# Combining expert rows inside the last expert, and projections ahead of the gates: a two-layer decoder step on one Trainium2 core

## The chip, the cores and the metric

The kernel runs on one core of one Trainium2 chip. Its engines are TensorE (PE), VectorE (DVE), ScalarE (ACT), GpSimd (POOL) and SyncE (SP). SP issues the loads of the weights, POOL the other transfers. The metric is the device time of one execution in microseconds, as the median of several runs.

## The reference, cut to what matters

520 tokens (512 of a prompt, 8 samples) pass two layers of width 1024. Each layer is a mixer, a feed-forward part and an input embedding p, with RMS norms around them. In the second layer the feed-forward part is a mixture of eight experts, of which each token uses two:

```python
gates = sum(one_hot(top_i) * top_p)            # two of 8 per token
for e in range(8):
    y = y + gates[..., e:e+1] * swiglu(h, wg[e], wu[e], wd[e])
x = x + rms_norm(y, norm_ffn_post)
gate = sigmoid(rms_norm(x, norm_ple) @ ple_w_gate)
x = x + gate * (p @ ple_w_proj)
```

All inputs are float32. The change is in the last lines: how y is put together for the tokens in layer 1, and when p @ ple_w_proj is computed.

## The kernel before, in words

Activations are kept transposed: 128 partitions by eight chunks of 520 tokens (x, acc). Dense matrix products split both factors into a rounded part and a remainder in PE's fast float32 format (whi and wlo by split(), h_hi and h_lo) and add three products; a matmul of 128 x 260 in that form is one instruction. A plain float32 matmul is two.

**The experts (layer 1).** The tokens of each expert are gathered into 160 slots (CAP): POOL scatters token rows to DRAM (xslot) by index (idxu), and loads the 160 rows of each expert back. Every expert has 30 weight slabs (E_SLABS): 11 pairs of gate and up, 8 of down. SP streams the slabs into a ring of 10; load number m waits until PE has read slab m - 10. In experts_by_slots() PE runs slab after slab with slab_slots(); gate slabs leave PSUM by ACT's Silu, up slabs by DVE's product (gs). A slab may start when the slab four before it has left its PSUM bank. For each down slab d, ACT or DVE copies the result to ytb, PE transposes it back to rows in rows_out() (lines 974 and 975), and rows_act() or rows_dve() copy the rows to ys0 and ys1; POOL stores them to DRAM (yslot). In the same place slots_in() transposes the rows of the next expert. If an expert had more rows than slots, experts_by_all() would run in place of this.

**After the last expert.** SP waits for the last slab, then loads two projection slabs (in_ple_w_proj) and the first two gate slabs. ACT and DVE split them, project_p() runs eight times on PE, and take_p() copies each result. Meanwhile POOL waits until all rows are stored and gathers, for five tiles t of 128 tokens (the last has 8), two rows per token (lines 649 and 650). ACT scales the first row by its gate (ctok), DVE adds the second, PE transposes the tile (line 1060), DVE adds it to acc in add_rows(). Only two tiles fit: POOL's third gather waits for DVE's first sum. Then ACT loads the table for logarithm and exponential, squares the eight chunks of acc, PE forms the means in norm(), root() makes the factor rn by Ln and Exp. normed() adds acc * rn to x on DVE and POOL, new_h() and low_h() make the next h, eight gate slabs run (slab()), and gated() multiplies by the projections.

Each engine runs its program in order, so the order of the work is written out by hand: where one engine needs another's result, it waits on a semaphore for a count, and everything behind it on that engine waits as well. The names that matter below: moe_done counts slabs by PE, act_out and dve_out what left PSUM, yx_t row transposes, ys_act and ys_dve row copies, y_back gathers, cb_a, cb_b, cb_t and cb_acc the steps of the combine.

Of the kernel before, what the change touches and what calls it, by code (L numbers as in the profile page):

```python
# [59 lines left out]
NSLOT = NE * CAP  # L60
SLICES = (2, 0)
# [30 lines left out]
def build(nc, A, O):  # L92
    ctx = ExitStack()
    with ctx:
# [21 lines left out]
        sq_sum = z[:, 12]  # L116
# [16 lines left out]
        with nc.sbuf_tensor("yrow", [P, 2, 2, DM], f32) as yrow, nc.sbuf_tensor("ctok", [P, 2, DM], f32) as ctok:  # L133
            pass
        with nc.sbuf_tensor("gu_hi", [P, FCH, TOK], f32r) as gu_hi, \
                nc.sbuf_tensor("gu_lo", [P, FCH, TOK], f32r) as gu_lo:
            pass
# [15 lines left out]
        with nc.sbuf_tensor("ys1", [P, DM], f32) as ys1:  # L153
            pass
# [22 lines left out]
        slot0 = sb("slot0", [P, 5])  # L177
        rt_col = sb("rt_col", [P, 5])
# [12 lines left out]
        def view(region, at, *shape):  # L191
# [3 lines left out]
            v = region[:, at:at + n]  # L195
            if len(shape) == 2:
                v = v.rearrange("p (a b) -> p a b", b=shape[1])
# [38 lines left out]

        def hn(k):

            return hn_a[:, k] if k < 6 else hn_b[:, k - 6]
# [29 lines left out]
        def two(ap):  # L269
# [4 lines left out]
        yslot = nc.dram_tensor("yslot", (NSLOT + 1, DM), f32).ap()  # L274
# [41 lines left out]
        acc0 = sem("acc0")  # L316
        hx_t, hx_ok, x_zero, rt_oh, rt_cnt, rt_idx, xs_scat, xs_in, xg_t, pk = (
            sem(s) for s in ("hx_t", "hx_ok", "x_zero", "rt_oh", "rt_cnt", "rt_idx", "xs_scat", "xs_in", "xg_t", "pk"))
        rwx_ok, rt_raw, rt_r, htok_ok, in0_ok, all_h = (
            sem(s) for s in ("rwx_ok", "rt_raw", "rt_r", "htok_ok", "in0_ok", "all_h"))  # L320
# [6 lines left out]
        y_back = [sem("y_back0"), sem("y_back1")]  # L327
# [45 lines left out]
        def _(sp):  # L373
# [27 lines left out]
            for L in range(DEPTH):  # L401
# [33 lines left out]
                loads(b + 1, PLE_P - 1, (b + 1) % 2, lambda s, i: cut(A["ple_w_gate"][L], i * 2 + s), kcs("ple"))  # L435
# [8 lines left out]
        def _(pool):  # L444
# [29 lines left out]
            for L in range(DEPTH):  # L474
# [126 lines left out]
                if L == 0:  # L601
# [6 lines left out]
                    for n in range(2):  # L608
                        half = yslot[NSLOT:NSLOT + 1, n * (DM // 2):(n + 1) * (DM // 2)]
# [6 lines left out]
                if L:  # L616
                    pool.wait_ge(r_ready, 5 * L + 3)
                    pool.memset(ytb[:, :, :], 0.0)
                    pool.memset(acc[:, :, :], 0.0).then_inc(acc0, 1)
# [22 lines left out]
                    pool.wait_ge(y_stored, 32 * (NE + 1))  # L642

                    for t in range(5):
                        n = P if t < TT else NB
                        if t >= 2:
                            pool.wait_ge(cb_b, t - 1)
                        for k in range(2):
                            pool.indirect_dma_start(out=yrow[0:n, t % 2, k, :], out_offset=None, in_=yslot[:, :],
                                                    in_offset=bass.IndirectOffsetOnAxis(ap=idxu[0:n, t, k:k + 1], axis=0),  # L650
                                                    bounds_check=NSLOT, oob_is_err=False).then_inc(y_back[t % 2], 16)
# [8 lines left out]
        def _(pe):  # L660
# [11 lines left out]
            def mean_of_sum(N, between=None):  # L672

                pe.wait_ge(sq_used, N * DC + DC - 1)
                for a in range(2):
                    mm(aux[:, a, 0:HALF], bcol(C_MEAN), two(sq_sum)[:, a], True, False)
# [6 lines left out]

            def norm(N):
                for c in range(DC):
                    mean(N, c)
# [200 lines left out]
            for L in range(DEPTH):  # L887
# [26 lines left out]
                if L:  # L914
                    pe.wait_ge(rwx_ok, 1)
# [13 lines left out]
                    pe.wait_ge(rt_raw, 1)  # L929
# [12 lines left out]
                    pe.wait_ge(rt_oh, 1)  # L942
# [26 lines left out]
                    def rows_out(e, d):  # L969

                        pe.wait_ge((act_out, dve_out)[d % 2], (e * E_SLABS + 2 * FCH + d) // 2 + 1)
                        if d >= 2:
                            pe.wait_ge((ys_act, ys_dve)[d % 2], e * DC // 2 + d // 2)
                        nc.tensor.transpose(aux[:, 2 + d % 2, 0:P], ytb[:, d % 2, 0:P], ident)  # L974
# [1113 lines left out]
```

## Time and profile before

| what | us |
|---|---|
| median of 3 runs | 1812.45 |
| lowest and highest | 1810.30, 1812.48 |
| the profiled execution | 1810.67 |
| its span, first to last instruction | 1808.9 |
| PE busy in the span | 1722.9 |
| ACT, DVE busy | 473.2, 579.6 |

The profiled execution is the one that all rows are from; its time is its span and 1.8 us around it. Times in rows are microseconds from the start of the span. Busy times of PE are modelled, and instructions overlap in it by their drains, so steps are better read from start to start.

### The profile page before, as it was taken

The numbers are of one execution on the slowest core, as the hardware profiler recorded it, in microseconds if no ns is written. First come the engines' busy times: TensorE is split into PE (matmuls) and PEld (weight loads), VectorE is DVE, ScalarE is ACT, GpSimd is POOL, SyncE is SP. The second block draws the span as 40 slices with busy tenths as digits, with TensorE's granted clock in tenths as the row PEclk, the third lists the DMA queues.
The fourth block names the chain that finished last, engine by engine and source line by source line (L and its number), as shares of the span: only waits on it lengthen the run. The fifth ranks groups of instructions, "written<-read, shape, count | busy, mean of one in ns | idle before, by whom it ended". The sixth has DMA issues, their size and how long they took to land.

```text
span 1808.9 us, 29442 instructions
## 1 busy us (share of the span) xinstructions
PE 1722.9 (95%) x12618; PEld 1619.7 (90%) x12618; DVE 579.6 (32%) x921; ACT 473.2 (26%) x836; POOL 258.1 (14%) x327
## 2 busy tenths in 40 slices
PE   7999998999999998899999799999999999999668
PEld 7877998999999997897789689999999999999658
DVE  3444535443344334643535500110101011010155
ACT  5232544222122334432334400110101101010242
POOL 5642211000000003054310220000000000000210
PEclk9999999999999999999999869999999999999879
DMA  4345361232222323223533257668686776965502
GB/s 164 83 86 117 76 207 59 93 102 97 77 88 91 113 64 98 70 72 89 111 77 107 92 177 258 225 226 279 198 289 216 244 249 205 300 195 197 168 17 90
DMA packets 70231, 260.69 MB, mean 144 GB/s; under 512 B 9849, under 2 KB 10369, under 8 KB 70097
## 3 DMA queue, kind: packets, MB, share of 16 engines
q1 hardware_dynamic: 56736, 219.52, 36.9%
q0 software_dynamic: 13376, 39.45, 8.3%
q8 instruction: 92, 1.51, 0.4%
q14 instruction: 27, 0.21, 0.0%
HBM read 237.20 MB, written 21.96 MB: 143 GB/s over the span
## 4 chain that ended last, share of the span: by engine, by line
PE 91%; DVE 4%; ACT 2%; DMA 1%; issue 1%; POOL 0%; ACTq 0%; DVEq 0%; SPq 0%; POOLq 0%
PE lin L662 77%; PE aux L662 12%; DVE h_lo L1536 1%; DVE zreg L1533 1%; PE aux L974 1%; DVE zreg L1536 1%; PE aux L966 1%; ACT h_hi L1098 1%; DMA yrow<-yslot,idxu 0%; DVE x L1533 0%; PE aux L975 0%; ACT htok L1098 0%; PE aux L965 0%; DMA wreg<-in_w_in_slabs 0%; DVE wlo L1533 0%
## 5 line engine op out<-in xcount | busy, mean ns | idle before, releaser
L662 PE MATMUL lin<-h_hi,whi 128*128 128x260 f32 x1616 | 432.8, 289 | 23.6 <-DVE h_lo L1536 23.6
L662 PE MATMUL lin<-h_lo,whi 128*128 128x260 f32 x1616 | 424.3, 284 | 0.0
L662 PEld LDWEIGHTS lin<-h_hi,whi 128*128 128x128 f32 x1616 | 308.3, 191 | 33.3 <-issue 27.6
L662 PE MATMUL lin<-h_hi,wlo 128*128 128x260 f32 x1616 | 327.8, 285 | 0.0
L662 PE MATMUL lin<-zreg,wreg 128*128 128x160 f32 x2304 | 321.6, 301 | 2.8 <-issue 2.8
L662 PEld LDWEIGHTS lin<-zreg,wreg 128*128 128x128 f32 x2304 | 317.2, 192 | 5.0 <-issue 4.9
L662 PEld LDWEIGHTS lin<-h_lo,whi 128*128 128x128 f32 x1616 | 307.8, 190 | 0.6
L662 PEld LDWEIGHTS lin<-h_hi,wlo 128*128 128x128 f32 x1616 | 251.2, 190 | 0.0
L1533 DVE TENSOR_TENSOR wlo<-wreg,whi 128x1024 fp32r<-128x1024 f32 (+1 forms) x140 | 180.7, 1291 | 96.3 <-ACT whi L1098 96.3
L1098 ACT ACTIVATE whi<-wreg 128x1024 fp32r<-128x1024 f32 (+1 forms) x140 | 152.1, 1090 | 74.5 <-DMA wreg<-in_ffn_w_down 26.8
L662 PE MATMUL lin<-region_b,wreg 128*128 128x160 f32 x1056 | 151.9, 300 | 0.0
L662 PEld LDWEIGHTS lin<-region_b,wreg 128*128 128x128 f32 x1056 | 145.0, 190 | 0.7
L1533 DVE TENSOR_TENSOR region_b<-zreg,lin 128x160 f32<-128x160 f32 x88 | 28.3, 322 | 342.7 <-PE lin L662 342.7
L1415 ACT ACTIVATE zreg<-lin 128x160 f32<-128x160 f32 x88 | 26.8, 304 | 347.7 <-PE lin L662 347.7
L1533 DVE TENSOR_TENSOR zreg<-lin,zreg 128x520 f32<-128x520 f32 x79 | 55.1, 698 | 156.5 <-PE lin L662 149.7
L472 POOL TENSOR_TENSOR x<-x,zreg 128x520 f32<-128x520 f32 x16 | 27.5, 1721 | 533.4 <-DVE zreg L1536 533.4
L662 PE MATMUL lin<-gu_hi,whi 128*128 128x260 f32 x352 | 92.0, 283 | 0.0
L662 PE MATMUL lin<-gu_lo,whi 128*128 128x260 f32 x352 | 91.9, 282 | 0.0
L640 POOL DMA_DIRECT2D yslot<-zreg x8 | 4.5, 561 | 606.2 <-DVE ys L1832 606.2
L662 PE MATMUL aux<-zreg,const 128*128 128x260 f32 (+1 forms) x216 | 66.3, 440 | 11.7 <-DVE h_lo L1536 8.0
L1098 ACT ACTIVATE zreg<-aux 128x128 f32<-128x128 f32 (+1 forms) x40 | 13.7, 342 | 224.4 <-PE aux L975 112.8
L662 PE MATMUL lin<-zreg,ring_more 128*128 128x160 f32 x512 | 72.2, 299 | 0.0
(280 smaller groups left out, 2281.8 us busy)
## 6 DMA issues: line engine op xcount, KB each, us to landing
wreg<-in_moe_w_gate SPq DMA_DIRECT2D x72, 512.0 KB, 4.2
wreg<-in_moe_w_up SPq DMA_DIRECT2D x72, 512.0 KB, 4.4
wreg<-in_moe_w_down SPq DMA_DIRECT2D x48, 704.0 KB, 5.2
wreg<-in_w_in_slabs SPq DMA_DIRECT2D x44, 512.0 KB, 3.5
wreg<-in_ffn_w_gate SPq DMA_DIRECT2D x22, 512.0 KB, 3.4
wreg<-in_ffn_w_up SPq DMA_DIRECT2D x22, 512.0 KB, 3.3
wreg<-in_ffn_w_down SPq DMA_DIRECT2D x16, 704.0 KB, 4.0
ring_more<-in_moe_w_down SPq DMA_DIRECT2D x16, 704.0 KB, 5.2
```

The lines of the kernel that those rows point to most:

```text
L472: pool.tensor_tensor(x[:, c], x[:, c], ut[:, 1], ALU.add).then_inc(x_pool, 1)
L640: pool.dma_start(yslot[e * CAP:e * CAP + P, :], ys0).then_inc(y_stored, 16)
L662: return nc.tensor.matmul(out, lhsT, rhs, start=start, stop=stop)
L966: nc.tensor.transpose(aux[:, k % 2, P:CAP], xs[0:CAP2, 1, k * P:(k + 1) * P], ident[0:CAP2, 0:CAP2]).then_inc(xg_t, 1)
L974: nc.tensor.transpose(aux[:, 2 + d % 2, 0:P], ytb[:, d % 2, 0:P], ident)
L1098: return nc.scalar.activation(out, in_, ACT.Copy, **k)
L1415: nc.scalar.activation(sg2[:, i % 2], lin[:, m % 4, 0:CAP], ACT.Silu).then_inc(act_out, 1)
L1533: return nc.vector.tensor_tensor(out, a, b, op)
L1536: return nc.vector.scalar_tensor_tensor(out=out, in0=a, scalar=s, in1=b, op0=op0, op1=op1)
```

## The change

It has these parts.
- The rows of experts 0 to 6 are gathered and combined while the last expert runs: POOL gathers after the seventh store, into three buffers (yrow(t)); a token whose row is the last expert's reads a row of zeros instead (idxg). ACT and DVE combine in place at i = 5 to 9 of the last expert's gate and up slabs, PE transposes a tile after slabs 12, 14, 16, 18 and 20 (combine()), DVE copies it to acc.
- The last expert's rows are not stored. places() and places_x() transpose a one-hot of tokens and slots (put7, put7x) and form each slot's gate (gcol). Each down slab's rows are scaled and split in a rounded part and a remainder (rows7_act(), rows7_dve()), put() multiplies them by the one-hot, put_in() adds the result to acc, and its square follows at once. 
- The table load moves ahead of the last down slabs. The means are formed from a running sum (mean_of_sum()) instead of eight products.
- SP loads the projection slabs and the first gate pair during the last down slabs. They are split there and in the tail. Projections 0 to 2 run between the last put()s and the means, 3 to 7 after the means and ahead of the gates.
- POOL's clearing of ytb and acc, and the waits for it, are gone; two spare semaphores are merged into others. The router gets six small DVE operations (slot7, idxg, gate7).
- The fallback experts_by_all() is fitted to the new counts.

The diff, cut to the last expert and what follows:

```diff
@@ SP
-                if L:
-                    sp.wait_ge(moe_done, NE * E_SLABS)
-                loads(b, 1, b % 2, lambda s, i: cut(A["ple_w_proj"][L], s), kcs("ple"))
-                loads(b + 1, PLE_P - 1, ...)
+                for i in range(PLE_P):
+                    for s in range(2):
+                        if L and i < 2:
+                            sp.wait_ge(moe_done, NE * E_SLABS - 8 + 4 * i + 2 * s)
+                        load(b + i, (b + i) % 2, s, ple(s, i), DC)
@@ POOL
-                    pool.memset(ytb[:, :, :], 0.0)
-                    pool.memset(acc[:, :, :], 0.0).then_inc(acc0, 1)
+                        if e == NE - 1:
+                            break
-                    pool.wait_ge(y_stored, 32 * (NE + 1))
+                    pool.wait_ge(y_stored, 32 * NE)
+                    pool.wait_ge(put_t, 1)
+                    pool.wait_ge(rt_idx, 2)
                     for t in range(5):
-                        if t >= 2:
-                            pool.wait_ge(cb_b, t - 1)
+                        if t >= 3:
+                            pool.wait_ge(cb_t, t - 2)
+                            pool.wait_ge(y_back[t % 3], 32)
@@ PE
+                    def places():
+                        pe.wait_ge(dve_out, (NE - 1) * E_SLABS // 2)
+                        for t in range(TT):
+                            nc.tensor.transpose(aux[:, 0, t * P:(t + 1) * P], in0[:, t, 0:P], ident)
+                        nc.tensor.transpose(aux[:, 1, 0:NB], in0[0:NB, TT, 0:P], ident[0:NB, 0:NB])
+                        nc.tensor.transpose(aux[0:CAP2, 1, NB:2 * NB], in0[0:NB, TT, P:CAP], ident[0:NB, 0:NB])
+                        for a, slots in enumerate((slice(0, P), slice(P, CAP))):
+                            for t in range(5):
+                                last = mm(aux[...], in0[0:n, t, slots], gate7[0:n, t:t + 1], t == 0, t == 4)
+                        last.then_inc(put_t, 1)
+                    def combine(t):
+                        pe.wait_ge(cb_b, t + 1)
+                        pe.wait_ge(put_ok, 2)
+                        if t:
+                            pe.wait_ge(cb_acc, t)
+                        for c in range(DC):
+                            last = nc.tensor.transpose(aux[...], yrow(t)[0:n, 0, c * P:(c + 1) * P], ident[0:n, 0:n])
+                        last.then_inc(cb_t, 1)
+                    def put(d):
+                        pe.wait_ge(ys_dve, (NE - 1) * DC // 2 + d + 1)
+                        pe.wait_ge(cb_acc, 5)
+                        if d:
+                            pe.wait_ge(oh_acc, d)
+                        for rows, slots in ((yhl, put7), (yxhl, put7x)):
+                            for part in range(2):
+                                for a in range(2):
+                                    last = mm(aux[:, a, 0:HALF], rows[:, part, d % 2], two(slots[:, :])[:, a], ...)
+                        last.then_inc(oh_t, 1)
...
+                                if e == NE - 1 and n == 2:
+                                    places()
+                                if e == NE - 1 and n == 6:
+                                    places_x()
+                                if e == NE - 1 and n >= 12 and n % 2 == 0:
+                                    combine(n // 2 - 6)
...
+                                if e == NE - 1 and d >= 2:
+                                    put(d - 2)
                         rows_out(NE - 1, DC - 1)
+                        project_p(1, 0)
+                        put(DC - 2)
+                        project_p(1, 1)
+                        put(DC - 1)
...
-                    for n in range(DC):
-                        project_p(1, n)
-                    for t in range(5):
...
-                if L:
-                    norm(5 * L + 3)
+                    project_p(1, 2)
+                    pe.wait_ge(oh_acc, DC)
+                    mean_of_sum(5 * L + 3)
+                    for n in range(3, DC):
+                        project_p(1, n)
@@ ACT, last expert (i over gate slabs, d over down slabs)
+                                if e == NE - 1 and 5 <= i < 10:
+                                    t = i - 5
+                                    act.wait_ge(y_back[t % 3], 32 * (t // 3 + 1))
+                                    cp(yrow(t)[0:n, 0, :], yrow(t)[0:n, 0, :], scale=gwt[0:n, t, 0:1]).then_inc(cb_a, 1)
+                            if e == NE - 1:
+                                log_exp_table()
...
+                                if e == NE - 1 and d in (4, 6):
+                                    split(ple_base(1), ple_base(1) % 2, d // 2 - 2, DC)
+                                if e == NE - 1 and d >= 3:
+                                    square_acc7(d - 3)
+                                if e == NE - 1 and d:
+                                    rows7_act(d - 1)
...
+                        rows7_act(DC - 1)
+                        split(ple_base(1) + 1, (ple_base(1) + 1) % 2, 0, DC)
+                        take_p(1, 0)
+                        square_acc7(DC - 3)
+                        square_acc7(DC - 2)
+                        take_p(1, 1)
+                        split(ple_base(1) + 1, (ple_base(1) + 1) % 2, 1, DC)
+                        square_acc7(DC - 1)
@@ DVE, last expert
+                                if e == NE - 1 and 5 <= i < 10:
+                                    dve.wait_ge(cb_a, t + 1)
+                                    stt(yrow(t)[0:n, 0, :], yrow(t)[0:n, 1, :], gwt[0:n, t, 1:2], yrow(t)[0:n, 0, :],
+                                        ALU.mult, ALU.add).then_inc(cb_b, 1)
                                 dve.wait_ge(moe_done, m + 1)
                                 tt(gs[:, i], sg2[:, i % 2], lin[:, m % 4, 0:CAP], ALU.mult).then_inc(dve_out, 1)
+                                if e == NE - 1 and i >= 6:
+                                    dve.wait_ge(cb_t, t + 1)
+                                    nc.vector.tensor_copy(acc[...], aux[...]).then_inc(cb_acc, 1)
...
+                                if e == NE - 1 and d in (5, 7):
+                                    split(ple_base(1), ple_base(1) % 2, d // 2 - 2, DC)
+                                if e == NE - 1 and d >= 3:
+                                    put_in(d - 3)
+                                if e == NE - 1 and d:
+                                    rows7_dve(d - 1)
...
+                        rows7_dve(DC - 1)
+                        put_in(DC - 3)
+                        add_squares(5 * L + 3, DC - 4)
+                        put_in(DC - 2)
+                        add_squares(5 * L + 3, DC - 3)
+                        add_squares(5 * L + 3, DC - 2)
+                        put_in(DC - 1)
+                    def put_in(d):
+                        dve.wait_ge(oh_t, d + 1)
+                        tt(two(acc[:, d]), two(acc[:, d]), aux[:, 0:2, 0:HALF], ALU.add).then_inc(oh_acc, 1)
+                        if d < DC - 3:
+                            add_squares(5 * L + 3, d - 1)
```

## Rows read from the trace of the kernel before

**Rows 1.** The page's part 1: busy time, share of the span, instructions.

```profile
PE 1722.9 (95%) x12618; PEld 1619.7 (90%) x12618; DVE 579.6 (32%) x921; ACT 473.2 (26%) x836; POOL 258.1 (14%) x327
```

**Rows 2.** The chain of waits in order of time: start, length, what.

```profile
1613.40 51.62 PE lin L662 x380
...
1681.18 0.11 PE aux L975
1681.29 3.00 PE lin L662 x22
...
1684.31 4.35 DMA wreg<-in_ple_w_proj
...
1691.05 14.40 PE lin L662 x96
...
1709.41 0.03 POOLq L649
...
1712.41 5.58 DMA yrow<-yslot,idxu
...
1731.37 8.77 PE aux L662 x32
...
1740.92 0.65 ACT zreg L1136
...
1762.73 40.26 PE lin L662 x336
```

**Rows 3.** Busy time of PE, PEld, DVE, ACT, POOL by stretch; granted clock, DMA share, GB/s.

```profile
1640.00:1650.00 10.00, 10.00 (x76) 10.00 (x75) 0.64 (x2) 0.61 (x2) 0.00 (x0) 1.00 0.92 305
...
1691.00:1697.00 6.00, 5.95 (x28) 5.95 (x29) 1.22 (x1) 2.00 (x3) 0.00 (x0) 0.51 0.47 189
...
1740.20:1758.40 18.20, 12.03 (x57) 10.60 (x57) 13.55 (x19) 11.19 (x18) 6.72 (x4) 0.81 0.01 1
```

**Rows 4.** PE's timeline: one-column matmuls, a combine tile, a pair of mean matmuls.

```profile
913.22 1.84 PE L662 MATMUL aux<-zreg,region_b 128*128 128x1 f32 x16
...
1723.04 1.63 PE L1060 MATMUL lin<-const,ctok 128*128 128x128 f32 x8 [0.54 <-DVE ctok L1536]
...
1758.40 1.14 PE L662 MATMUL aux<-zreg,const 128*128 128x260 f32 x4 [0.89 <-DVE h_lo L1536]
```

**Rows 5.** ACT's timeline: an expert-row copy, two projections, a combine tile.

```profile
1684.53 0.28 ACT L1098 ACTIVATE zreg<-aux 128x128 f32<-128x128 f32 x1 [3.12 <-PE aux L975]
...
1698.28 0.61 ACT L1098 ACTIVATE region_y<-lin 128x520 f32<-128x520 f32 x1 [1.01 <-PE lin L662]
1699.72 0.60 ACT L1098 ACTIVATE region_y<-lin 128x520 f32<-128x520 f32 x1 [0.83 <-PE lin L662]
...
1718.01 1.15 ACT L1098 ACTIVATE ctok<-yrow,gwt 128x1024 f32<-128x1024 f32 x1 [8.10 <-DMA yrow<-yslot,idxu]
```

**Rows 6.** DVE's timeline: ytb copy, split, combine, a gate product read from PSUM.

```profile
1684.32 0.33 DVE L1852 COPY ytb<-lin 128x160 f32<-128x160 f32 x1 [2.52 <-PE lin L662]
...
1689.77 1.23 DVE L1533 TENSOR_TENSOR wlo<-wreg,whi 128x1024 fp32r<-128x1024 f32 x1 [4.12 <-ACT whi L1098]
...
1709.94 1.28 DVE L1536 SCALAR_TENSOR_TENSOR ctok<-yrow,gwt,ctok 128x1024 f32<-128x1024 f32 x1 [0.56 <-ACT ctok L1098]
...
1768.49 0.70 DVE L1533 TENSOR_TENSOR zreg<-lin,zreg 128x520 f32<-128x520 f32 x1 [0.60 <-PE lin L662]
```

**Rows 7.** POOL's timeline: the seventh and eighth store, two gather issues.

```profile
1615.03 0.50 POOL L641 DMA_DIRECT2D yslot<-ys  x1
...
1686.79 0.50 POOL L641 DMA_DIRECT2D yslot<-ys  x1
1697.02 1.08 POOL L649 DMA_INDIRECT yrow<-yslot,idxu  x1 [9.72 <-DMA yslot<-ys]
...
1710.15 1.96 POOL L649 DMA_INDIRECT yrow<-yslot,idxu  x1 [8.13 <-DVE ctok L1536]
```

**Rows 8.** DMA issues from 1538 to 1575: size, median us to landing.

```profile
zreg<-xslot POOLq DMA_DIRECT2D x1, 512.0 KB, 7.0
```

More of the change, by code:

```diff
@@ L153, in build @@
         with nc.sbuf_tensor("ys1", [P, DM], f32) as ys1:
+            pass
+        with nc.sbuf_tensor("yhl", [P, 2, 2, P], f32r) as yhl, nc.sbuf_tensor("yxhl", [P, 2, 2, P], f32r) as yxhl:
             pass
@@ L235, in build, with yrow @@
         assert a <= 2 * DC * TOK
+        yrow_a, a = view(ry, 0, 2, 2, DM)
+        assert a + 2 * TOK <= FCH * TOK
+        yrow_b, a = view(ra, 5 * DM, 2, DM)
+        def yrow(t):
+            return yrow_b if t % 3 == 2 else yrow_a[:, t % 3]
         def hn(k):
@@ new lines, in places_x @@
+                    def places_x():
+                        pe.wait_ge(put_ok, 1)
+                        for t in range(TT):
+                            last = nc.tensor.transpose(aux[0:CAP2, 0, t * P:(t + 1) * P], in0[:, t, P:CAP], ident)
+                        last.then_inc(put_t, 1)
+                    def combine(t):
+                        n = P if t < TT else NB
+                        pe.wait_ge(cb_b, t + 1)
[3 more added lines that the diff above has]
+                        for c in range(DC):
+                            last = nc.tensor.transpose(aux[:, c // 4, (c % 4) * P:(c % 4) * P + n],
+                                                       yrow(t)[0:n, 0, c * P:(c + 1) * P], ident[0:n, 0:n])
+                        last.then_inc(cb_t, 1)
@@ new lines, in put @@
+                    def put(d):
[6 more added lines that the diff above has]
+                                for a in range(2):
+                                    last = mm(aux[:, a, 0:HALF], rows[:, part, d % 2], two(slots[:, :])[:, a],
+                                              rows is yhl and part == 0, rows is yxhl and part == 1)
+                        last.then_inc(oh_t, 1)
@@ L1395, in _, with square_acc7 @@
                     last.then_inc(htok_ok, 1)
+                    def square_acc7(d):
+                        act.wait_ge(oh_acc, d + 1)
+                        square(5 * L + 3, d, two(acc[:, d]))
                     def slots_act(e, k):
@@ L1445, in experts_by_all @@
                                 cp(spare[:, :], epsc[:, :]).then_inc(ys_act, 1)
+                        log_exp_table()
+                        for n in range(3):
+                            act.wait_ge(y_back[n], 32 if n == 2 else 64)
+                        for s in range(2):
+                            split(ple_base(1), ple_base(1) % 2, s, DC)
+                        split(ple_base(1) + 1, (ple_base(1) + 1) % 2, 0, DC)
+                        take_p(1, 0)
+                        for d in range(DC):
+                            square_acc7(d)
+                        take_p(1, 1)
+                        split(ple_base(1) + 1, (ple_base(1) + 1) % 2, 1, DC)
                     for k in range(0, DC, 2):
@@ L1495, in _ @@
                             stream(b + GU_P, DOWN_P, kcs("down"), kcs("ple"), square_acc, ACT.Ln)
-                if L:
-                    log_exp_table()
-                    for c in range(DC):
-                        square(5 * L + 3, c, two(acc[:, c]))
                 b = ple_base(L)
@@ L1503, in _ @@
                     take_p(0, 0)
-                root(5 * L + 3)
-                split(b + 1, (b + 1) % 2, 1, DC)
-                if L == 0:
+                    root(3)
+                    split(b + 1, (b + 1) % 2, 1, DC)
                     take_p(0, 1)
                     take_p(0, 2)
-                new_h(2 * L + 2, 64 + 8 * L, added(2 * L + 1), 5 * L + 4, lambda c: take_p(0, c + 3) if L == 0 and c < 5 else None)
+                    new_h(2, 64, added(1), 4, lambda c: take_p(0, c + 3) if c < 5 else None)
+                else:
+                    take_p(1, 2)
+                    root(5 * L + 3)
+                    take_p(1, 3)
+                    take_p(1, 4)
+                    new_h(2 * L + 2, 64 + 8 * L, added(2 * L + 1), 5 * L + 4, lambda c: take_p(1, c + 5) if c < 3 else None)
                 root(5 * L + 4)
@@ L1891, in experts_by_all @@
                                 nc.vector.tensor_copy(gtmp[:, 0, 0:1], fits[:, 0:1]).then_inc(ys_dve, 1)
+                        for d in range(DC):
+                            dve.drain()
+                            nc.vector.tensor_copy(gtmp[:, 0, 0:1], fits[:, 0:1]).then_inc(oh_acc, 1)
+                        for s in range(2):
+                            split(ple_base(1), ple_base(1) % 2, s, DC)
+                        for d in range(1, DC - 1):
+                            add_squares(5 * L + 3, d)
                     for k in range(1, DC, 2):
```

168 lines of the change are left out of this document (96 added, 72 removed).

## The prediction

> **What bounds the kernel now.** I read the page first: TensorE (PE) is busy for nearly the whole span [rows 1], so elsewhere only added or removed PE work would count. The exception is the end, so I read the chain of waits from the last expert on [rows 2]. Up to 1684.3 it is PE alone: 16-instruction gate/up slabs and 22-instruction down slabs at some 0.136 us an instruction, 2.17 and 3.0 us a slab. Then it leaves PE: load of the projection slab (4.35), its split, eight projections (14.4), copies, the gather of the expert rows (5.58 for one of its landings), combine, table load, 8.77 of squares and means, root. The norm factor is ready at 1741.57, the end of the last ACT step. So 57.3 us lie between the last slab and that factor, and no expert or gate matmul is among them. From the factor to the end nearly the same work follows before and after. The granted clock by stretch [rows 3] is 1.00 (2.4 GHz) while experts run and 0.51 (1.2 GHz) just after the load wait.
>
> **Part 1: the tail, walked.** Zero is 1684.0, when PE has issued the last slab (modelled end 0.3 later). Prices: a transpose 0.11 [rows 2]; a projection or put(): ACT's evictions come 1.44 apart for twelve matmuls, 0.12 each, so put() with eight takes 0.95 [rows 5]; an expert-row copy on ACT starts about 0.33 after its transposes were issued (1684.2, 1684.53) and takes 0.28 [rows 5], with its 32-row half some 0.45, an estimate, on DVE I take 0.5; ytb copy 0.33, put_in() like the gate product that reads PSUM, 0.70, split 1.23 [rows 6]; a square like the Exp of the same size, 0.65 [rows 2]; a pair of fp32 mean matmuls 1.14 with 0.3 of drain, so 0.85 [rows 4].
> - rows_out(6) 0.2, ACT's rounded rows 1.0, DVE's remainders 1.5, then DVE's ytb copy of slab 7, which now queues behind them: 1.85. rows_out(7) 2.1. put(5) (0.2 to 1.2) lies beside this.
> - rows 7 rounded 2.9, remainders 3.4, put_in(5) 4.1 (in order behind them, although put(5) is long done). project_p(0), 2.1 to 3.5, is hidden in this.
> - put(6) 5.05, project_p(1) 6.5, put(7) 7.45, put_in(7) 8.35, last square 8.95. project_p(2), 7.45 to 8.9, is hidden; so are take_p(0) and (1), both splits of the first gate pair on ACT and DVE, put_in(6) and the square sums. The tightest is ACT's second split, which ends at 8.3, just before the last square can start; without that cover it would cost up to 1.0.
> - mean_of_sum 10.6, then Ln and Exp: before it took 1.43 from the end of the means to the factor, so 12.3.
>
> So the factor comes at 1696.3 instead of 1741.57: **-45.3**. The projection load has no price left: SP issues it as the down slabs begin, into ring slots already read, and 4.35 passes under the four slabs ahead of its split. The table load and five of the eight squares now lie under the down slabs. Ends for this walk: 10 if the DVE waits overlap better, 16 if each hand-over costs 0.4 more.
>
> Projections 3 to 7 stand ahead of the gates and take 7.2 on PE after the means, where PE was busy for 12.0 of 18.2 [rows 3]: DVE and ACT set that stretch. take_p(3) and (4) fit into the 2.1 between factor and first x; take_p(5) to (7) come between ACT's h_hi and can hold DVE's next h_lo by 0.1 to 0.3 each: **+0.4**. Later gate slabs (40.26 [rows 2]) are unchanged.
>
> **Part 2: PE work put into the last expert.** places(): four transposes, two small ones and ten one-column fp32 matmuls; eight of these took 1.84 with their tail [rows 4], so 2.1 and 0.55. places_x(): 0.44. combine(): 8 x 0.11 four times, and some 0.8 for the 8-row one; the old combine took 1.63 for eight [rows 4], but with the clock low for part of it, so that is the upper end. put(0) to put(5): 5.7. Sum 13.1, all of it on the path, since PE sets the end there: **+13.1** (11 to 17, the upper end if combine goes by its old rows). Nothing at the clock: it is 1.00 there with transposes between the slabs [rows 3].
>
> Each down slab of the last expert then takes 3.0 + 0.22 + 0.95 = 4.2 on PE. DVE has at most a split, put_in, add_squares, a pair and a ytb copy, 3.3; ACT a split, a square, a pair and a copy, 2.4. Neither binds. ytb copies and put_in stand one slab ahead of what PE needs.
>
> **Part 3: the gathers in the last expert.** POOL now waits for the seventh expert's store; from the eighth's issue at 1686.8 to the first gather at 1697.0 it took 10.2, and the seventh's was issued at 1615.0 [rows 7], so the first gather goes out near 1625. Six issues of 1.3 follow, each landing 5.6 after its issue [rows 2], t=0 at about 1634, t=2 at 1642 or some us later beside the weight stream. ACT wants t=0 at 1638 and t=2 at 1647 (slab 0 of the last expert ends by 1613.4 [rows 2], slab 2i 2.17 x 2i later, and 3.1 to 5 more for the inserted work). ACT and DVE may wait a further 4 there, since PE runs four slabs ahead of their results. Queued behind such a wait is ACT's next Silu, DVE's next gate product, and behind these PE.
>
> Tightest is t=3: POOL waits for combine(0), at 1643.2, POOL's start, two issues and a landing took 8.6 in the tail (1709.4 to 1718.0 [rows 2]), so 1652.0; ACT is ready for it at 1652.7, then 1.15 [rows 5] and 1.28 [rows 6], ready 1655.3; PE wants combine(3) at 1657.9. Spare: 3.3 (2.6 of it PE's, 0.7 ACT's). A POOL-queue load beside the weight stream landed in 7.0 [rows 8], 1.5 more than the gathers alone; the DMA engines are 0.92 busy there [rows 3]. Bounds: no stall, or 9 (landing doubled to some 14). I take **+1**, nearer the 7.0. One gather issue took 1.96 and not 1.0 [rows 7] while DVE ran its 1.28 combine: that can happen in here too, and is inside the spare.
> On this the Trainium skill, page "SBUF — State Buffer", section "SBUF: two separate sides", has a rule against the change: a DVE instruction with two SBUF inputs and a GpSimd instruction that reads SBUF exclude each other for the whole instruction. The trace agrees (1.96 beside 1.28); by the rule each of the ten issues could wait a full combine, some 2.6 for t=3, which alone would nearly use up its spare.
>
> The weights: from 1625 on six slabs of 512 KB, eight of 704 KB and 4.3 MB of gathered rows are to be moved, 13.4 MB; at the 305 GB/s of [rows 3] that is 44 us, until 1669, while the last down slab is wanted past 1690. No stall.
>
> **Part 4: the router stage** gains six small DVE operations of some 0.2 and loses POOL's clearing of acc. DVE's next work there waits for PE for several us, so nothing. ACT's two zeroing copies in the first expert lie under 4 us of idle time. Gone too are the last store and PE's waits for a clear.
>
> **Sum.** -45.3 + 0.4 + 13.1 + 1 = -30.8. The profiled execution has 1810.67 (span 1808.9), so 1779.9; its time is 1.8 under the median of the three runs, 1812.45. I say **1780**. Ends: 47.3 saved and 11 added, 1774.4, and some 2 less if the first gate slab, whose stretch has a clock of 0.81 now [rows 3], runs at 1.00; 41.3 saved, 17 added, 9 of stalls, from the median, 1797. Range **1772 to 1797**. A measurement can tell 0.2%, 3.6 us.
>
> **Rivals.**
> 1. **Late gathers** (0.13). They stall combine(2) to combine(4) by 5 to 15 together: 1784 to 1794. For it: 0.92 busy DMA, the doubled issue, POOL's turn through combine(0). Against: 4 us of lead on ACT, 3.3 on PE. The rule on DVE and GpSimd above would bring this case.
> 2. **Low clock in the tail** (0.05). If PE's gaps of about 1 us let the clock fall to 0.51 as after the load wait [rows 3], the 7.9 of PE work on the walk doubles: 1788. Against: the gap ahead of that fall was 6 us.
> 3. **Starved gathers, slower** (0.04). The gathers get nothing while weights stream. combine(0) then waits until the stream is done at about 1655 (SP's last slabs are asked for one ring ahead of PE), the 8.6 of a gather and 2.4 of copies: 1666 in place of 1642, 24 lost; t=3 goes round once more in the same way, the 8.6 and 2.4 behind up to ten slabs, 20 more. 1780 + 44 - 1 = 1823. It decides from 31 us of stalls on. Against: POOL's loads and stores land beside the same stream [rows 8].
> 4. **It does not do what it says**: were the last expert's rows to overflow 160 slots, the fallback loop would run; the trace of before runs the slot path on the same inputs. Chance nil.
>
> **Numbers.** The forecast's own case (1772 to 1788) 0.77, rivals 0.13, 0.05 and 0.04, 0.01 between. The first three are all faster: 0.95; slower 0.04; the same 0.01, a stall of just 27 to 35.
>
> **What would show it.** Right: in the chain of waits, some 12 us between the last expert slab and the norm's Exp, no gather and no load in it; last expert longer by 14, PE without waits on yrow; no table load between. Wrong: PE waiting for DVE's combine in the gate/up slabs, for split or put_in in the down slabs, a granted clock of 0.5 in the tail, or put() far over 0.95.

## The result, and the profile after

The changed kernel takes 1785.8 us (median; 1781.9 to 1788.6) where the kernel before takes 1811.6 beside it: ratio 0.9856, 95% interval 0.9836 to 0.9877, some 26 us faster. The forecast was 1780 in a range of 1772 to 1797. Two more sets of runs gave 0.9868 (0.9849 to 0.9887) and 0.9861 (0.9836 to 0.9886). The profiled execution after is one of 1784.76, with a span of 1783.0; before it was 1810.67 and 1808.9.

First the page's part 1, as in [rows 1]:

```profile
PE 1721.7 (97%) x12688; PEld 1620.7 (91%) x12688; DVE 591.9 (33%) x950; ACT 477.5 (27%) x852; POOL 255.0 (14%) x323
```

TensorE has 70 instructions more and 1.2 us less of busy time, in a span that is 25.9 us shorter: what went is nearly all idle time. Where it went is read from the chain of waits (start, length, what), which answers to [rows 2]; here from the start of the last expert on:

```profile
1612.52 2.41 PE lin L685 x16
...
1644.26 0.89 PE aux L1026 x8
...
1648.14 8.34 DMA region_y<-yslot,idxg
1656.50 1.16 ACT region_y L1172
...
1658.89 0.31 DVE region_b L1656
1659.20 1.15 DVE zreg L1985
...
1660.48 1.07 PE aux L1026 x8
...
1695.91 2.99 PE lin L685 x22
...
1703.15 1.18 PE aux L685 x8
1704.33 1.45 PE lin L685 x12
1705.77 0.95 PE aux L685 x8
1706.73 2.22 issue
1708.95 2.97 PE lin L685 x12
1711.91 2.01 PE aux L685 x8
1713.92 2.90 PE lin L685 x24
...
1736.82 40.26 PE lin L685 x336
```

And the last step of the root on ScalarE, in its timeline, whose end is the norm factor r:

```profile
1714.72 0.64 ACT L1210 ACTIVATE zreg<-zreg 128x520 f32<-128x520 f32 x1
```

The chain holds no load, no gather and no table load between the last expert slab and r. The slab is issued at 1695.91 + 2.99 = 1698.90, and r is ready at 1715.36. I cut both profiles at the same four marks of this chain:

| stretch | before | after | difference | forecast |
|---|---|---|---|---|
| start of the span to the last expert | 1610.77 | 1612.52 | +1.75 | 0 |
| last expert, to the issue of its last slab | 73.52 | 86.38 | +12.86 | +14.1 |
| last slab to r | 57.28 | 16.46 | -40.82 | -45.3 |
| r to the end of the span | 67.33 | 67.64 | +0.31 | +0.4 |
| sum | 1808.90 | 1783.00 | -25.90 | -30.8 |

The first row can't be told from the spread of single executions. In the runs below, with the same code up to the first expert, the last expert starts anywhere from 1610.1 to 1613.3 (branches_swapped, with its longer entry, left out), and both values lie in that range. One difference is the granted clock: from 800 to 900 us it was 1.00 before and 0.97 after. The row that matters is the third. In the chain TensorE does nothing for 2.22 us between put(7) and project_p(2), and nothing that the profile knows of ends that wait. Then project_p(2) takes 2.97 where project_p(1), the same twelve matmuls, took 1.45. The windows of that place (busy time of PE, PEld, DVE, ACT and POOL, then granted clock, DMA share, GB/s), which answer to [rows 3]:

```profile
1705.00:1706.80 1.80, 1.73 (x15) 1.52 (x13) 1.41 (x4) 1.63 (x3) 0.00 (x0) 1.00 0.04 9
1706.80:1709.00 2.20, 0.05 (x1) 0.06 (x1) 0.66 (x1) 1.20 (x2) 0.00 (x0) 0.98 0.03 7
1709.00:1712.00 3.00, 3.00 (x13) 3.00 (x14) 2.36 (x2) 0.05 (x1) 0.00 (x0) 0.50 0.04 8
1712.00:1714.00 2.00, 2.00 (x10) 1.69 (x10) 0.00 (x0) 0.59 (x2) 0.00 (x0) 0.92 0.00 0
```

The clock is at its upper level until the pause, and at 0.50, which is 1.2 GHz, for the 3 us behind it. VectorE pauses at the same place:

```profile
1706.77 0.70 DVE L1656 TENSOR_TENSOR zreg<-zreg,aux 128x520 f32<-128x520 f32 x1 [0.29 <-PE aux L685]
1709.62 2.36 DVE L1656 TENSOR_TENSOR wlo<-wreg,whi 128x1024 fp32r<-128x1024 f32 x2 [2.16 <-issue]
```

In the code put(7) and put_in(7) are the last steps of `experts_by_slots()`. Behind them the engines leave the branch `If(fit == 1)` and pass over the code of `experts_by_all()`, the fallback that is not used. The only traffic in the pause is this line of the DMA queues of 1706.7 to 1709:

```profile
q14 instruction: 2, 0.02, 2.6%
```

**Theory:** leaving the branch is a jump over the whole fallback to instructions that are not at hand, it costs 2 us, and the idle time brings the clock down. In the kernel before, by its code, the same jump lay under the wait for the projection's load, 4.35 us [rows 2]. **Rival:** a wait that the profile does not show, or a clock that falls for the loose work of put(6) and put(7).

### The profile page after: what moved, and what is told of

Same layout as the page of the kernel before. It is cut to its first block and busy times, and to the rows that moved or that the text cites. A ratio compares the mean times of both kernels' runs of the same rounds, so it can differ in the third digit from the quotient of the medians.

```text
span 1783.0 us, 29654 instructions
## 1 busy us (share of the span) xinstructions
PE 1721.7 (97%) x12688; PEld 1620.7 (91%) x12688; DVE 591.9 (33%) x950; ACT 477.5 (27%) x852; POOL 255.0 (14%) x323
## 5 line engine op out<-in xcount | busy, mean ns | idle before, releaser
L685 PE MATMUL lin<-gu_hi,wlo 128*128 128x260 f32 x352 | 71.1, 283 | 0.0
L685 PEld LDWEIGHTS lin<-zreg,ring_more 128*128 128x128 f32 x512 | 70.4, 190 | 0.0
```

What stands on the lines that cost most here:

```text
L685: return nc.tensor.matmul(out, lhsT, rhs, start=start, stop=stop)
```

## The experiments

Twelve runs. The third column is the last expert from its start to the issue of its last slab, the fourth the wait of TensorE for the fourth set of rows inside it, the fifth the time from the last slab to r. All but the medians and ratios is of the profiled executions.

| run | median, us; ratio to before (95%) | last expert | wait | slab to r |
|---|---|---|---|---|
| the changed kernel | 1785.8; 0.9856 (0.9836-0.9877) | 86.38 | 0.6 | 16.46 |
| after_again | 1787.1; 0.9868 (0.9849-0.9887) | 90.37 | 2.9 | 16.76 |
| after_third | 1787.1; 0.9861 (0.9836-0.9886) | 89.10 | 3.2 | 16.38 |
| pe_means_inside | 1787.7; 0.9870 (0.9849-0.9891) | 90.81 | 3.3 | 12.49 |
| rest_inside | 1784.1; 0.9846 (0.9826-0.9865) | 91.25 | 3.7 | 12.49 |
| branches_swapped | 1786.1; 0.9871 (0.9852-0.9891) | 89.10 | 1.6 | 12.49 |
| short_fallback | 1783.3; 0.9852 (0.9833-0.9871) | 90.64 | 3.1 | 12.48 |
| loads_early_alone | 1807.9; 0.9988 (0.9978-0.9999) | 73.5 | none | 54.49 |
| five_buffers | 1783.0; 0.9849 (0.9832-0.9866) | 85.64 | none | 16.51 |
| put_rounded_rows_only | 1786.2; 0.9867 (0.9850-0.9884) | 86.48 | 3.0 | 15.83 |
| five_buffers_rounded_only | 1780.7; 0.9841 (0.9825-0.9858) | 83.24 | none | 15.84 |
| all_three | 1780.1; 0.9835 (0.9817-0.9852) | 85.65 | none | 11.66 |
| best | 1777.5; 0.9815 (0.9801-0.9829) | 87.34 | none | 10.87 |

Single executions of one kernel differ by up to 15 us and the intervals are 4 to 9 us wide, so a change of 2 to 4 us is read from the stretches. In five of the twelve executions with the change (after_again, pe_means_inside, branches_swapped, short_fallback, best) 10 us of the last expert ran at a granted clock of 0.83 to 0.86, about 1.7 us more. No edit of these runs goes with it, but a piece of the change does: the clock falls to 0.50 for some 3 us, without a pause of TensorE that the profile shows, within 1 us behind the one-column matmuls of places() (20 instructions in 1.78 us). In the other seven it stays at 1.00 behind the same matmuls, and the kernel before, which has none of them, is at 1.00 in this place. The same 10 us of the changed kernel and of after_again (columns as in [rows 3]; 76 matmuls against 66):

```profile
1622.52:1632.52 10.00, 10.00 (x76) 9.93 (x76) 0.64 (x2) 1.30 (x7) 6.08 (x6) 1.00 0.75 279
```

```profile
1620.61:1630.61 10.00, 10.00 (x66) 9.94 (x65) 0.64 (x2) 1.02 (x7) 6.05 (x6) 0.86 0.78 257
```

**The changed kernel again.**

> The changed kernel itself, so that the variants have its time from the same chip. Four executions of it spread from 1781.9 to 1788.6 us; expected 1784 to 1787, ratio to the kernel before 0.985 to 0.987. In its trace again: TensorE rests about 2.2 us between put(7) and project_p(2) under 'issue', project_p(2) takes 3.0 us at a granted clock of 0.50 to 0.55, and the factor r is taken up about 16.5 us after TensorE has issued the last expert slab.

The pause was 2.36 us and r came at 16.76. Project_p(2) took 2.16 and not 3.0, at a mean clock of 0.74, and the means 2.94 at 0.61, where they had 2.01. The wait for the fourth rows, which I had not asked about, was 2.9 in place of 0.6.

**Where the branch ends: four edits.** First, TensorE's work up to the means stands inside both branches:

```diff
                         experts_by_slots()
+                        to_means()      # project_p(1, 2), wait oh_acc, mean_of_sum
                     with pe.Else():
                         experts_by_all()
+                        to_means()
...
-                    project_p(1, 2)
-                    pe.wait_ge(oh_acc, DC)
-                    mean_of_sum(5 * L + 3)
```

> TensorE alone: project_p(2), the wait for the last put_in and the pair of means stand inside both branches, so that TensorE leaves the branch after the means and not between put(7) and project_p(2). Theory (leaving the branch costs TensorE 2.2 us as it jumps over the unused fallback, and the pause brings the clock down): the gap before project_p(2) is gone, project_p(2) takes 1.45 us as the two before it, the factor r comes at 12 to 13.5 us after the last slab in place of 16.5, and the time falls by 3 to 4.5 us against the changed kernel. The jump's 2.2 us then stand behind the means, beside the root and r. Rival (the gap is a wait for ScalarE or VectorE that the profile doesn't name, or the clock falls for the loose work of the puts): the gap or the slow project_p(2) stays where it is, and the time is within 1 us of the changed kernel.

The chain of this run:

```profile
1710.37 1.44 PE lin L685 x12
1711.81 1.75 PE aux L685 x8
1713.56 2.09 issue
1715.65 4.66 PE lin L685 x24
```

The pause went to where the branch now ends, behind the means: project_p(2) takes 1.44, the means 1.75, and r comes 4 us sooner, at 12.49. The time did not fall with it, which I had not expected: now project_p(3) and project_p(4) stand behind the pause and take 4.66 in place of 2.90. ScalarE has to take both up before its first h_hi, which starts 5.83 us behind r; it was 2.11. The span from r to the end grew from 67.64 to 71.4. The pause is cheap only where the engine would wait anyway.

Second, everything of the layer behind the experts inside both branches, on all three engines:

```diff
                     with pe.If(fit == 1):
                         experts_by_slots()
+                        rest()          # all of layer 1 that follows
                     with pe.Else():
                         experts_by_all()
+                        rest()
```

> All of layer 1 behind the experts stands inside both branches on TensorE, ScalarE and VectorE, so that no engine leaves a branch before the output is computed. Theory: the gap of 2.2 us is gone on TensorE and on VectorE, the clock stays at 1.00 from the last slab to r, r comes 12 to 13.5 us after the last slab, and the time is 3 to 4.5 us below the changed kernel, at most 0.5 us from the run with the means alone inside. Rival (a wait that is not shown): no change within 1 us, or the gap comes back at the same place.

```profile
1711.43 0.97 PE aux L685 x8
1712.39 1.44 PE lin L685 x12
1713.83 1.75 PE aux L685 x8
```

No pause, no slow matmul, r at 12.49, and from r to the end 68.07. So neither put(6) nor put(7) brings the clock down. The median is 3.0 below that of after_again, with intervals that overlap; in the profile its wait for rows of 3.7 us, with a clock of 0.57 in the 4 us behind it, hides the gain.

Third, the branches in the other order:

```diff
-                    with pe.If(fit == 1):
-                        experts_by_slots()
-                    with pe.Else():
-                        experts_by_all()
+                    with pe.If(fit == 0):
+                        experts_by_all()
+                    with pe.Else():
+                        experts_by_slots()
```

> The fallback stands first in the code on TensorE, ScalarE and VectorE (if it doesn't fit: fallback, else: by slots), so that the work by slots falls through at its end, and the jump over the fallback is at the entry. Theory: no gap before project_p(2), r at 12 to 13.5 us after the last slab, and the step at the entry before the first expert grows from 1.25 to about 2 us or more: some 2 to 4 us below the changed kernel. Rival (the cost lies in the end of a branch as such and not in the jump over the fallback): the gap of about 2 us stays before project_p(2), the time is within 1 us of the changed kernel.

TensorE's first expert slab in its timeline, with the idle time ahead of it; first here, then in the changed kernel:

```profile
1070.99 2.48 PE L685 MATMUL lin<-zreg,wreg 128*128 128x160 f32 x8 [6.74 <-issue]
```

```profile
1067.99 2.47 PE L685 MATMUL lin<-zreg,wreg 128*128 128x160 f32 x8 [1.69 <-issue]
```

The pause at the end is gone (r at 12.49), and the one at the entry has grown from 1.69 to 6.74, far more than the 2 us that I had put there. So 4.0 are won at one end and 5.05 lost at the other, and the time stays.

That a jump over the fallback costs this much was shown so far by moving it. The last run shortens it:

```diff
                     with pe.Else():
-                        experts_by_all()
+                        project_p(1, 0)   # ACT: a table load; DVE: one add_squares
```

> The changed kernel with the fallback's body cut to one step on each engine (twelve matmuls on TensorE, a table load on ScalarE, one add on VectorE), so that leaving the branch jumps over a few instructions in place of the whole fallback loop; the fallback, which these inputs don't take, is left out. Theory A (what costs the 2.0 to 2.5 us is a jump to instructions that are far off and have to be fetched): the pause before project_p(2) falls under 0.5 us on TensorE and VectorE, no instruction packet moves in it, r comes 12.4 to 13 us after the last slab, and the time is 2 to 5 us below the changed kernel. Theory B (a taken jump costs that much whatever its length): the pause stays at 2.0 us or more and r at 16.4 to 16.8. At the entry, where the jump is not taken, both expect the 1.7 us of every run.

```profile
1706.16 1.44 PE lin L685 x12
1707.60 0.97 PE aux L685 x8
1708.56 1.44 PE lin L685 x12
```

The branch ends where it did, the jump is still taken, and the pause is gone: project_p(2) follows put(7) at once, r comes at 12.48. The median, 1783.3, is 2.4 to 3.8 below the three of the changed kernel, which are from other sets of runs, with overlapping intervals. Theory A holds in the pause and in r; its detail of the packets does not: two instruction packets move between 1706 and 1711.7 here as well, only TensorE does not stand still for them. The Trainium skill, page "Runtime: NRT & Kernel Launch", section "Instruction fetch mechanics", says that instructions are fetched ahead in sequence only, and that a taken branch to a target outside what is held stalls until its page has been fetched; the runs agree, with 2.0 to 2.7 us on TensorE at the long jump and none at the short one. That a fetch is what fills the time is argued from this and not shown by itself.

**The loads alone, on the kernel before.**

```diff
-                if L:
-                    sp.wait_ge(moe_done, NE * E_SLABS)
-                loads(b, 1, b % 2, lambda s, i: cut(A["ple_w_proj"][L], s), kcs("ple"))
...
+                        if L and i < 2:
+                            sp.wait_ge(moe_done, NE * E_SLABS - 8 + 4 * i + 2 * s)
+                        load(b + i, (b + i) % 2, s, ple(s, i), DC)
```

> The kernel before with one piece of the change alone: SP lets the four loads of the projection and of the first gate pair start during the last expert's down slabs. Theory of the prediction (the tail of the kernel before is bounded by the last expert's store and the gathers behind it, and the early loads only pay because the gathers left): the wait of 4.35 us for the load is gone and the projections end some 6 us sooner, but the first combine waits longer for its gather; r moves from 57.6 us after the last slab to 54 to 57, and the time falls by 0 to 3.5 us. Rival (the load wait and the split were a large part of what the change won, and stand alone): the whole 5.6 us or more are won, r at 52 or below.

```profile
1690.88 1.08 POOL L653 DMA_INDIRECT yrow<-yslot,idxu  x1 [3.43 <-DMA yslot<-ys]
...
1706.73 1.31 POOL L653 DMA_INDIRECT yrow<-yslot,idxu  x1 [10.85 <-DVE ctok L1540]
```

R came 54.49 us after the last slab in place of 57.28, 2.8 sooner, and the time fell by 0.1 to 2.2 parts in a thousand. The size is as expected, the reason is not. The last projection is copied from PSUM 3.4 us sooner (1702.06 for 1705.48), where I had 6. With no load beside it the last store lands sooner, and the first gather starts at 1690.88 after a wait of 3.43, not 9.72 [rows 7]. But the third gather then waits 10.85 us for the first combine, and this stands in ScalarE's and VectorE's order behind eight projections and the splits. So on the kernel before the loads alone are worth some 3 of the 41 us. TensorE's wait ahead of the projections, 3.52 here, ends 1.5 us behind the split that project_p(0) needs (1687.31), which fits the jump out of the branch; that the jump is the reason was not tested on this kernel. The opposite, late loads in the changed kernel, was not tried: there the splits of the projection stand on ScalarE ahead of rows that the last slabs wait for.

**The fourth set of rows.** Five row buffers in place of three:

```diff
-            return yrow_b if t % 3 == 2 else yrow_a[:, t % 3]
+            return (yrow_a[:, 0], yrow_a[:, 1], yrow_b, yrow_c[:, 0], yrow_c[:, 1])[t]
...
-                            pool.wait_ge(cb_t, t - 2)
```

> The changed kernel with five row buffers in place of three: the fourth and fifth gather wait for no combine. Theory (the wait of TensorE for the fourth rows, 0.6 us in the first profile and 1.6 to 3.7 in four others, comes from a gather that is issued late since its buffer is busy): that wait is gone, the last expert (its start to the issue of its last slab) takes 85.5 to 86 us, and the time falls by 0.5 to 3.5 us against the changed kernel. Rival (the gathers' landings themselves are slow beside the weight stream, whenever they start): the wait stays at 1 us or more, no change in time.

POOL's timeline, the fourth set's two gather issues and the fifth's first in the changed kernel, then the fourth set's with five buffers:

```profile
1645.91 1.92 POOL L672 DMA_INDIRECT region_y<-yslot,idxg  x1 [14.98 <-PE aux L1026]
1648.14 0.99 POOL L672 DMA_INDIRECT region_y<-yslot,idxg  x1 [0.30 <-issue]
1651.24 1.75 POOL L672 DMA_INDIRECT region_y<-yslot,idxg  x1 [2.11 <-PE aux L1026]
```

```profile
1629.04 1.00 POOL L672 DMA_INDIRECT region_a<-yslot,idxg  x1 [0.58 <-issue]
1630.35 0.99 POOL L672 DMA_INDIRECT region_a<-yslot,idxg  x1 [0.30 <-issue]
```

Counted from the start of the last expert they go out 15 us sooner (18.5 for 33.4), TensorE waits for no rows, and the last expert takes 85.64. The median, 1783.0, is 2.7 to 4.1 below those of the changed kernel, with overlapping intervals. With three buffers the same landing took 8.34 us in the changed kernel's first profile, and in after_again and rest_inside:

```profile
1647.91 10.65 DMA region_y<-yslot,idxg
```

```profile
1648.91 11.54 DMA region_y<-yslot,idxg
```

This spread is the wait's: 0.6, 2.9 and 3.7 us. The landing stays slow with five buffers too (10.8 is the median of the six gathers into these buffers); it only starts early enough.

**Is the added work on TensorE's path?** Half of each put left out:

```diff
-                            for part in range(2):
-                                for a in range(2):
-                                    last = mm(aux[:, a, 0:HALF], rows[:, part, d % 2], ...)
+                            for a in range(2):
+                                last = mm(aux[:, a, 0:HALF], rows[:, 0, d % 2], ...)
```

> The changed kernel with half of each put left out: the rounded rows alone go to the tokens, their remainders don't (that part of the computation is missing). Theory (TensorE's added work in the last expert lies on the path, since the down slabs there are bound by TensorE): each put takes 0.48 to 0.5 us in place of 0.96, the last expert takes 2.5 to 3 us less (six puts inside it), the tail about 1 us less, and the time falls by 3 to 4.5 us. Rival (in the down slabs the weight stream sets the pace and the puts lie beside it): the last expert stays within 0.8 us of 86.4 us and TensorE waits for loads in their place.

The time did not show it: a wait of 3.0 us for rows stood in this profile, and the median is that of the changed kernel within the interval. So once more, without that wait:

> Five row buffers, and of each put the half with the rounded rows alone (the remainders are left out of the computation). With the rounded rows alone in three buffers, the wait for the fourth rows (3.0 us in that profile) hid what the halved puts won; without that wait it must show. Theory (the puts lie on TensorE's path): the last expert takes 83.0 to 83.5 us where five buffers with whole puts took 85.64, r comes at 15.7 to 16.0 after the last slab, and the time is 2.5 to 3.5 us below five buffers alone: 1779.5 to 1781. Rival (something else, the weight stream first, sets the pace): the last expert stays above 85 us.

```profile
1690.44 0.49 PE aux L685 x4
1690.93 2.99 PE lin L685 x22
```

The last expert takes 83.24 us against 85.64: 2.40, five puts (the sixth lies behind the last slab) of 0.48. The median is 2.4 lower than that of five buffers, from another set of runs, with overlapping intervals; the stretch is what shows that TensorE sets the pace there.

**Together.** The rest inside both branches, five buffers, and on VectorE:

```diff
+                        put_in(DC - 3)
                         rows7_dve(DC - 1)
-                        put_in(DC - 3)
```

> A version meant to be the best: the rest of the layer inside both branches, five row buffers, and VectorE's put_in(5) ahead of the last rows7_dve. Theory: no wait for the fourth rows, no gap on leaving the branch, clock at 1.00 from the last slab to r; r at 11.5 to 12.5 us after the last slab (12.5 with the old order); against the changed kernel 4 to 7 us less, 1779 to 1782 us, ratio to the kernel before 0.982 to 0.985. Rival (what is won before r is given back between r and the first gate slab, as in the run with the means alone inside): within 2 us of the changed kernel.

R comes at 11.66, so the new order is worth 0.8, and nothing is given back behind it: from r to the end it takes 68.1 us. Then also the last ytb copy ahead of rows7_dve(6), beside the changed kernel on one chip:

> The three edits together, and on VectorE the last slab's copy to ytb ahead of rows7_dve(6), so that the last rows are turned sooner. Theory: r at 10.9 to 11.4 us after the last slab (11.66 without this edit), the last expert at 85.6 us, no wait for rows; 5 to 8 us below the changed kernel of the same call, 1778 to 1781 us. Rival (put(6) and put(7) are bound by ScalarE's and VectorE's rows and not by when project_p(0) starts): r stays at 11.6 us.

> The changed kernel a third time, beside the two below on one chip. Expected 1784 to 1788 us; the wait for the fourth rows again somewhere between 0.5 and 4 us, r 16.4 to 16.8 us after the last slab.

```profile
1699.92 0.97 PE aux L685 x8
...
1701.11 1.46 PE lin L685 x12
1702.57 0.95 PE aux L685 x8
```

TensorE goes from put(5) to project_p(0) and from there to put(6) without a wait, and r comes at 10.87. The last expert took 87.34 and not 85.6, with the low clock behind places(). This version takes 1777.5 us, 0.9815 (0.9801 to 0.9829), beside 1787.1 and 0.9861 (0.9836 to 0.9886) of the changed kernel: it is below both kernels, and the intervals don't overlap.

## Why the prediction came out as it did

The forecast was faster by 30.8 from the profiled execution; it came to 25.9. By the table: 4.5 too much for the tail and 1.75 ahead of the last expert that no edit explains, less 1.2 too much for the last expert and 0.1 behind r: 4.9.

- **The tail, -45.3: right in mechanism, 4.5 short.** The step that failed is "project_p(2), 7.45 to 8.9, is hidden". It costed the matmuls, but not that TensorE and VectorE leave a branch ahead of them. In its place: 2.22 us of pause, 1.5 more for project_p(2) at the lower clock and 0.3 more for the means, 4.0 in all. The four runs with that pause moved or gone give 12.48 to 12.49, where the walk has 12.0 on the table's mark (its zero was 0.3 earlier). Its steps before the pause stand: on the same mark put(6) was walked to start at 3.8 and started at 4.25.
- **TensorE's work in the last expert, +13.1: right in mechanism, 1.0 too much.** Without any wait for rows it took 85.64 - 73.52 = 12.1. The 1.0 is put(5), which was counted twice: the walk has it beside the steps of the tail, and the +13.1 adds it to the path. It ran behind the last slab, where TensorE waits for rows anyway. The other puts are on the path, as the halved ones showed. The combine's transposes took 0.89, as priced at 0.11 each. "Nothing at the clock" held in seven profiles of twelve; in the other five the fall behind places() cost 1.7.
- **The gather's stall, +1: right within its bounds of 0 to 9, but too low for the usual run.** It was 0.6 in the profile of the result and 1.6 to 3.7 in seven others with three buffers. One term that was off is the landing: I took 7.0 [rows 8], and it took 8.3 to 11.5 beside the weight stream. The other is the spare. In all eight profiles the wait is the landing less 7.8, while 3.3 above a landing of 5.58 would have borne 8.9. The walk left out that combine(3) also waits for the copy of the third tile, which VectorE takes up behind the fourth combine and a gate product (0.31 and 1.15 in the chain above).
- **The rule on the shared port** (the Trainium skill, page "SBUF — State Buffer", section "SBUF: two separate sides"): agreed again. Two of the ten issues started beside a combine of VectorE with two inputs and took 1.92 and 1.75, the others 0.92 to 1.08; 0.8 to 0.9 more each, part of the spare. With five buffers all ten lie ahead of the combines and take 0.92 to 1.08.
- **+0.4 behind r: right**, 0.31.
- **The rivals.** Late gathers (stalls of 5 to 15) did not come, though the waits reached 3.7. Starved gathers: no, and in the last expert TensorE waited for no weights (the slabs and rows add up to 13.2 MB and not 13.4, which changes nothing). The low clock in the tail did come, at 0.50 as I had put it, but on 3 us and not on 7.9 of work, since it followed the one pause and not the short gaps between the puts: with the pause gone the clock stayed at 1.00 there.

## What to carry to other kernels

A branch can cost where it ends as well as where it starts: here, with a long untaken part behind it, TensorE stood still for 2.0 to 2.7 us when it left it, and a wait that used to cover this may be the one that the next change removes. So end a branch where the engine waits anyway, or with the rest of the program inside it. And where gathers run beside a weight stream, buffers that let them start early are worth more than a close estimate of their landing.

## What the runs showed of the hardware that was not expected

- A jump over the same code cost 2.0 to 2.7 us on TensorE at the end of the branch, and at the entry, with the branches swapped, 5.05 us more than the untaken one (6.74 against 1.69). Why the two differ stays open; at the entry POOL's loads of expert rows ran beside it. VectorE paid 2.16 at the end of the branch in the changed kernel, but in loads_early_alone, at the end of the branch of the kernel before, its pause was 0.29 and ScalarE had none. Why the price is not always paid was not tested.
- A pause of 2.1 to 2.2 us on TensorE was followed by a granted clock of 0.50 over 3 us (the changed kernel) and 0.64 over 4.7 (pe_means_inside); after one of 2.67 us in five_buffers_rounded_only it stayed at 1.00. After the wait of 3.7 us for rows it was 0.57 over 4 us, after waits of 2.9 to 3.3 us in five other profiles it stayed at 1.00, and waits of 0.6 never showed in it. Behind the one-column matmuls of places() it fell without any pause, in five profiles of twelve. So one profile is not enough to price the clock at such a place.
- The store of the last expert landed 6.3 us sooner (a wait of 3.43 for 9.72) once the loads of the projection and the gate no longer ran beside it.
